# Second layer's attention heads: exponentials and values in rounded halves, all lower halves by VectorE

## What is computed

```python
def one_block(qi):
    s = jnp.einsum('bqhgd,bkhd->bhgqk', qi, k, preferred_element_type=jnp.float32) * scale
    p = jax.nn.softmax(s, axis=-1)
    return jnp.einsum('bhgqk,bkhe->bqhge', p.astype(v.dtype), v)
```

## Time and profile before

| | us |
|---|---|
| median of three runs | 3668.6 (3667.87 to 3674.9) |
| profiled execution, its own time | 3685.8 |
| its span, first to last instruction | 3683.6 |
| heads of the second layer, first score product to last exponential | 2247.2 to 2647.6 |
| TensorE busy | 3453.5 |
| VectorE busy | 1712.7 |
| GpSimd busy | 785.5 |
| ScalarE busy | 734.8 |

### The profile page before, as it was taken

One profiled execution on the slowest core, in us unless ns is written; L12 is line 12 of the kernel. 1 busy time (PEld: TensorE's weight loads), 2 busy tenths in 40 slices (PEclk: granted clock), 3 DMA queues, 4 the chain that ended last, 5 costly groups with the idle time before them and its releaser, 6 DMA issues. The chain is left out here.

```text
span 3683.6 us, 47585 instructions
## 1 busy us (share of the span) xinstructions
PE 3453.5 (94%) x17824; PEld 2975.6 (81%) x17824; DVE 1712.7 (46%) x2862; ACT 734.8 (20%) x1334; POOL 785.5 (21%) x430
## 2 busy tenths in 40 slices
PE   6898899998989999999979988999898999999998
PEld 3787655556889999999969875555587999999998
DVE  1645456663185555555564364333225343333433
ACT  2322243333120000000032123433312000000001
POOL 1211111112222222222113111111221222222220
PEclk8898899999999999999989988999999999999999
DMA  5243433413112222122214334212120111111111
GB/s 186 71 140 108 135 101 111 121 52 88 43 58 77 64 75 68 57 76 65 62 27 134 118 119 101 55 39 58 52 81 29 35 46 46 34 46 40 40 34 51
DMA packets 306201, 271.11 MB, mean 74 GB/s; under 512 B 65778, under 2 KB 268292, under 8 KB 306100
## 3 DMA queue, kind: packets, MB, share of 16 engines
q1 hardware_dynamic: 277492, 234.36, 22.0%
q10 hardware_dynamic: 28608, 35.40, 2.7%
HBM read 221.81 MB, written 48.02 MB: 73 GB/s over the span
## 5 line engine op out<-in xcount | busy, mean ns | idle before, releaser
L1737 PE MATMUL ps<-h_hi,w_hi 128*128 128x384 f32 (+1 forms) x3072 | 1066.5, 347 | 78.2 <-DVE h_lo L1345 63.8
L1738 PE MATMUL ps<-h_lo,w_hi 128*128 128x384 f32 (+1 forms) x3072 | 1045.5, 340 | 0.0
L1739 PE MATMUL ps<-h_hi,w_lo 128*128 128x384 f32 (+1 forms) x3072 | 1045.5, 340 | 0.0
L1737 PEld LDWEIGHTS ps<-h_hi,w_hi 128*128 128x128 f32 (+1 forms) x3072 | 581.2, 189 | 94.2 <-issue 82.8
L1738 PEld LDWEIGHTS ps<-h_lo,w_hi 128*128 128x128 f32 (+1 forms) x3072 | 581.2, 189 | 11.5 <-issue 1.0
L1739 PEld LDWEIGHTS ps<-h_hi,w_lo 128*128 128x128 f32 (+1 forms) x3072 | 580.1, 189 | 3.2
L1658 DVE SCALAR_TENSOR_TENSOR x<-ps,lmod,x 128x384 f32<-128x384 f32 (+2 forms) x768 | 369.5, 513 | 332.9 <-PE ps L1739 332.8
L1562 DVE TENSOR_REDUCE neg_max<-ps 128x1 f32<-128x1152 f32 (+1 forms) x216 | 266.8, 1239 | 275.5 <-PE ps L2013 266.1
L1696 DVE TENSOR_TENSOR wk<-ps,wk 128x384 f32<-128x384 f32 x132 | 73.6, 558 | 688.9 <-PE ps L1739 684.6
L1252 ACT ACTIVATE wk<-ps 128x384 f32<-128x384 f32 x132 | 64.7, 492 | 1498.8 <-PE ps L1739 1482.5
L1186 ACT ACTIVATE p_t<-ps 128x512 f32<-128x512 f32 (+1 forms) x456 | 264.4, 580 | 482.3 <-PE ps L1739 256.0
(11 more groups left out here) (253 smaller groups left out, 4145.7 us busy)
## 6 DMA issues: line engine op xcount, KB each, us to landing
w_stage<-in_w_ffn_gate SPq DMA_DIRECT2D x44, 512.0 KB, 3.7
w_stage<-in_w_ffn_up SPq DMA_DIRECT2D x44, 512.0 KB, 3.8
w_stage<-in_w_ffn_down SPq DMA_DIRECT2D x44, 512.0 KB, 3.6
f_buf<-in_w_ada SPq DMA_DIRECT2D x176, 128.0 KB, 2.1
ada_buf<-in_w_ada SPq DMA_DIRECT2D x36, 512.0 KB, 6.6
s_in<-ev_p ACTq DMA_DIRECT2D x66, 192.0 KB, 2.2
w_stage<-in_w_in SPq DMA_DIRECT2D x24, 512.0 KB, 3.8
ada_w<-in_w_ada SPq DMA_DIRECT2D x4, 2048.0 KB, 17.2
```

The costliest lines, as they stand in the source:

```text
L1737: nc.tensor.matmul(out, wh, xh, start=first, stop=False)
L1738: nc.tensor.matmul(out, wh, xl, start=False, stop=False)
L1739: return nc.tensor.matmul(out, wl, xh, start=False, stop=last)
```

## The change

Only the second layer's heads change (`SPLIT_LAYERS = (1,)`); the first layer keeps its code.

- ScalarE takes two exponentials of each score tile, one written rounded (`p_hi`), one in full (`p_full`), into rings of three slots. TensorE may reuse the scores' bank after the second.
- VectorE subtracts: `p_lo = p_full - p_hi`, once a step (`p_low`). It also rounds and subtracts the values of the next head (`v_halves`, step 3) and makes the lower halves of the next head's queries and keys (`lows`, step 1), which were GpSimd's. The next head's rounding (`highs`) comes in step 0 behind that step's `p_low`; the reductions come one in each of the steps 5 to 13, each ahead of the step's `p_low`.
- TensorE: `products` is two rounded products (upper and lower half of the values by `p_hi`), `product_low` a third (upper half of the values by `p_lo`), issued one step later and behind the next step's `products`.
- GpSimd has nothing in these heads but the weight tiles behind them.
- The loops over pairs in this layer are written out.

```diff
+                    if l in SPLIT_LAYERS:
+                        st = split_step(y, i)
+                        slot = st % 3
+                        if st >= 3:
+                            act.wait_ge(lo_done, st - 2)
+                        nc.scalar.activation(p_hi[:, slot, 0:w], s_bank(half, i)[:, 0:w], ACT.Exp).then_inc(exp_done, 1)
+                        nc.scalar.activation(p_full[:, slot, 0:w], s_bank(half, i)[:, 0:w], ACT.Exp).then_inc(exp_full, 1)
+                        return
...
-                with pool.Fori(0, HEADS) as p:
-                    lows_mla(l * NHEADS + 2 * p)
-                    lows_gqa(l * NHEADS + 2 * p + 1)
+                if l not in SPLIT_LAYERS:
+                    with pool.Fori(0, HEADS) as p:
+                        lows_mla(l * NHEADS + 2 * p)
+                        lows_gqa(l * NHEADS + 2 * p + 1)
...
+                def lows(y, mla):
...
+                    for (lo, full, hi), done in zip(pieces, (q_low, k_low)):
+                        nc.vector.tensor_tensor(lo, full, hi.bitcast(F32), ALU.subtract).then_inc(done, 1)
+
+                def v_halves(p, half, first=False):
...
+                    nc.vector.tensor_copy(hi[:, :, 0:VD], raw[:, :, 0:VD]).then_inc(v_high, 1)
+                    dve.wait_ge(v_high, n + 1)
+                    nc.vector.tensor_tensor(lo[:, :, :], raw[:, :, 0:VD], hi[:, :, 0:VD].bitcast(F32), ALU.subtract)\
+                        .then_inc(v_done, 1)
+
+                def p_low(y, half, i):
...
+                    dve.wait_ge(exp_full, st + 1)
+                    if st >= 3:
+                        dve.wait_ge(pv_mm, y * STEPS + i - 2)
+                    nc.vector.tensor_tensor(p_lo[:, slot, 0:w], p_full[:, slot, 0:w], p_hi[:, slot, 0:w].bitcast(F32),
+                                            ALU.subtract).then_inc(lo_done, 1)
+
+                def pair_split(p, first=False, last=False):
+                    for half in range(2):
+                        y = l * NHEADS + 2 * p + half
+                        more = not (half and last)
+                        for i in range(STEPS):
+                            t = i - MAX_AT - 1
+                            if more and 0 <= t < MAX_TILES:
+                                max_tile(y + 1, t)
+                            p_low(y, half, i)
+                            if more and i == 0:
+                                highs(y + 1, p + half, half == 1)
+                            if more and i == 1:
+                                lows(y + 1, half == 1)
+                            if more and i == 3:
+                                v_halves(p + half, 1 - half, first=first and not half)
...
+                if l in SPLIT_LAYERS:
+                    lows(l * NHEADS, True)
+                    v_halves(0, 0, first=True)
...
                     if not first:
-                        pe.wait_ge(exp_done, st - 1)
+                        if l in SPLIT_LAYERS:
+                            pe.wait_ge(exp_full, split_step(y, i) - 1)
+                        else:
+                            pe.wait_ge(exp_done, st - 1)
...
+                    if l in SPLIT_LAYERS:
+                        _, vh, vl = v_half[half]
+                        slot = split_step(y, i) % 3
+                        nc.tensor.matmul(ps[0:VD + 1, GROUP_BANK[j], 0:w], vh[:, kt, 0:VD + 1], p_hi[:, slot, 0:w],
+                                         start=(i in (0, 9, STEPS - 1)), stop=False)
+                        nc.tensor.matmul(ps[0:VD, GROUP_BANK[j], 0:w], vl[:, kt, :], p_hi[:, slot, 0:w],
+                                         start=False, stop=False)
+                        return
...
+                def product_low(y, half, i):
...
+                    pe.wait_ge(lo_done, split_step(y, i) + 1)
+                    nc.tensor.matmul(ps[0:VD + 1, GROUP_BANK[j], 0:w], v_half[half][1][:, kt, 0:VD + 1],
+                                     p_lo[:, split_step(y, i) % 3, 0:w], start=False, stop=(i + 1 in GROUP_END))\
+                        .then_inc(pv_mm, 1)
...
                             products(y, p, half, i, first and not half)
+                            if l in SPLIT_LAYERS:
+                                if i:
+                                    product_low(y, half, i - 1)
+                                elif half or not first:
+                                    product_low(y - 1, 1 - half, STEPS - 1)
```

More of the change, by code:

```diff
@@ L243 @@
 MACS = 2 * DK
+SPLIT_LAYERS = (1,)
 LATE_HERE = 9
@@ L356, in build @@
             ("neg_max", [P, 16], F32))
+        p_full = place("p_full", [P, 3, 512], F32, ring_at + 4096)
+        p_hi = place("p_hi", [P, 3, 512], F32R, ring_at + 4096 + 3 * 2048)
+        p_lo = place("p_lo", [P, 3, 512], F32R, ring_at + (RING + 1) * 4096)
+        vm_hi, vm_lo, vg_hi, vg_lo = phase(
+            EVB + 6 * T * 4 + 4 * KEYS * 4 + 3 * 1024 + 2 * LAT * 4 + (HL + P) * 4,
+            ("vm_hi", [P, KT, VD + 8], F32R), ("vm_lo", [P, KT, VD], F32R),
+            ("vg_hi", [P, KT, VD + 8], F32R), ("vg_lo", [P, KT, VD], F32R))
+        v_half = ((mv, vm_hi, vm_lo), (gv, vg_hi, vg_lo))
         rope_x, rope_t0, swap = phase(EVB + 6 * T * 4 + 4 * KEYS * 4, ("rope_x", [P, N_ROPE, GW], F32),
@@ L442, in build @@
         f_mac, f_mm, f_ev = sem("f_mac"), sem("f_mm"), sem("f_ev")
+        exp_full, lo_done, v_high, v_done = sem("exp_full"), sem("lo_done"), sem("v_high"), sem("v_done")
         late_mac, late_mm, late_ev = sem("late_mac"), sem("late_mm"), sem("late_ev")
@@ L718, in load_v @@
                 def load_v(hh, dst, src, loaded):
-                    if hh >= 2:
+                    if hh >= 2 and l in SPLIT_LAYERS:
+                        sp.wait_ge(v_done, SPLIT_LAYERS.index(l) * NHEADS + hh - 1)
+                    elif hh >= 2:
                         sp.wait_ge(pv_mm, (l * NHEADS + hh - 1) * STEPS)
@@ L1180, in _, with split_step @@
                 r_store(R_NORMED - 1)
+                def split_step(y, i):
+                    return (y - (l - SPLIT_LAYERS.index(l)) * NHEADS) * STEPS + i
                 def exp_step(y, half, i):
@@ L1226, in _ @@
                 pair(0, first=True)
-                with act.Fori(1, 5) as p:
-                    pair(p)
+                if l in SPLIT_LAYERS:
+                    for p in range(1, 5):
+                        pair(p)
+                else:
+                    with act.Fori(1, 5) as p:
+                        pair(p)
                 pair(5, last=True)
@@ L1598, in ada_sums @@
                             ins.then_inc(late_mac, 1)
-                def pair(p, last=False):
+                def lows(y, mla):
+                    dve.wait_ge(q_high, y + 1)
+                    dve.wait_ge(k_high, y + 1)
+                    if mla:
+                        pieces = ((mq_lo[:, :], qst_m[:, :], mq_hi[:, :]), (mk_lo[:, :], kst_m[:, :], mk_hi[:, :]))
+                    else:
+                        pieces = ((ga[64:P, :], qst_g[64:P, :], ga[64:P, :]),
+                                  (kb[0:64, :], kst_g[0:64, :], ka[0:64, :]))
+                    for (lo, full, hi), done in zip(pieces, (q_low, k_low)):
+                        nc.vector.tensor_tensor(lo, full, hi.bitcast(F32), ALU.subtract).then_inc(done, 1)
@@ new lines, in v_halves @@
+                def v_halves(p, half, first=False):
+                    raw, hi, lo = v_half[half]
+                    n = SPLIT_LAYERS.index(l) * NHEADS + 2 * p + half
+                    dve.wait_ge(vg_loaded if half else vm_loaded, (l * HEADS + p + 1) * 16)
+                    if not first:
+                        dve.wait_ge(pv_mm, (l * NHEADS + 2 * p + half - 1) * STEPS)
+                    nc.vector.tensor_copy(hi[:, :, 0:VD], raw[:, :, 0:VD]).then_inc(v_high, 1)
+                    dve.wait_ge(v_high, n + 1)
+                    nc.vector.tensor_tensor(lo[:, :, :], raw[:, :, 0:VD], hi[:, :, 0:VD].bitcast(F32), ALU.subtract)\
+                        .then_inc(v_done, 1)
@@ new lines, in p_low @@
+                def p_low(y, half, i):
+                    st = (y - (l - SPLIT_LAYERS.index(l)) * NHEADS) * STEPS + i
+                    slot = st % 3
+                    _, w, _ = step_of(i)
+                    dve.wait_ge(exp_full, st + 1)
[3 more added lines that the diff above has]
+                                            ALU.subtract).then_inc(lo_done, 1)
@@ L1601, in pair @@
+                def pair(p, first=False, last=False):
+                    if l in SPLIT_LAYERS:
+                        pair_split(p, first, last)
+                        return
                     for half in range(2):
@@ L1616, in _ @@
                 nc.vector.memset(kst_m[96:97, :], 1.0).then_inc(att_const, 1)
-                nc.vector.memset(mv[:, :, VD:VD + 1], 1.0).then_inc(att_const, 1)
-                nc.vector.memset(gv[:, :, VD:VD + 1], 1.0).then_inc(att_const, 1)
+                for raw, hi, _ in v_half:
```

(34 more changed lines are left out.)

2 lines of the change are left out of this document (added).

## The result

The changed kernel takes 3682.7 us (median of nine, 3681.31 to 3684.93); the kernel before, beside it, 3669.8. The ratio is 1.0029, 95% interval 1.0017 to 1.0041: slower by about 0.3%. The forecast was 3675, and the time lies inside the range of 3662 to 3690; the change itself cost 12.9 us, twice the 6.1 of the sum. The direction and the mechanism in the GQA heads were right; of the terms, several were not.

The account below looks back on a forecast made before the run. TensorE (busy 94%) was taken as the bound, except in the reductions' ring with VectorE. Heads +0.6, entry +2.0 and clock +3.5 us sum to +6.1 on the median 3668.6, say 3675; range 3662 to 3690.

Parts of the forecast that it names:

- The mechanism: In a head's first steps VectorE's queue becomes the bound: TensorE waits for `p_low` 2, until 7.10 us after the first exponential.
- A: From a head's first exponential to its first reduction: 9.76 us forecast in GQA heads (+1.56), 10.20 in MLA heads (+0.83).
- B: The seven 2.24 us intervals between a head's eight large reductions, a ring of VectorE and TensorE; forecast gain and loss 0.
- The fast rival: VectorE is no bound at the head's start, its subtractions running at the pace of casts: 3650 us; chance 10%.
- The pass: On TensorE the full product of the values, 4 × 0.22 us, becomes three rounded ones: one pass of 0.22 less.
- C: From a head's last large reduction to the next head's first exponential: net -0.86 us a head, both kinds.
- VectorE's list in MLA heads: From 1.14 us after the first exponential, 5.96 of VectorE work until `p_low` 2 ends at 7.10; MLA heads net 0.
- The entry: Before the first head's scores, `lows` on VectorE run beside GpSimd's weight splits: 0 to +3.3 us, taken as +2.0.
- The clock: Standstills of 2.2 to 2.4 us in five GQA heads lower TensorE's clock: +3.5 us, bounds 0 and 7.5.
- rival of eleven falls: TensorE's clock falls in each of eleven heads, for longer, once MLA standstills pass some 2 us: 3690 us; chance 12%.
- a ring at half clock: In GQA heads the reductions' ring falls to the lower clock, 3.2 against 2.24 us a step: 3713 us; chance 4%.
- ScalarE: Two exponentials a step take 0.98 us, under TensorE's 1.10 and 1.32; rival, they don't overlap: 3680 us, chance 6%.

## Why the prediction was right, and where it was not

**The mechanism** in the GQA heads is the one forecast. `p_low` 2 of GQA head 7 ended at 7.09 after the first exponential (2502.76 and 0.69, less 2496.36), forecast 7.10; A of GQA heads without a clock fall is 9.77, forecast 9.76. B is unchanged. The spread `lows` took the standstills of both kinds of head away, so the cause is shown and not only argued. The fast rival fell with the widths: the subtractions took 1.35 and 1.49, as forecast.

**The pass: mis-sized.** I took 0.22 for a rounded product and for the pass saved. A product of 64 or 65 columns comes after 0.23, a GQA step lasts 1.16, not 1.10, and the saving is 0.16 a step. I had divided 1.32 by six as if the full form's four passes and the rounded ones were equal; the row was of the full form and of 128-column products only. Hence C gains 0.63 and 0.78 (0.86 forecast) and the last head 2.4 (2.9), about 2.0 us less in all. Of the 0.24 that the late small reduction was to cost, 0.10 came (1.88 less 1.78).

**VectorE's list in MLA heads: mis-sized.** A of MLA heads is 10.47 in place of 10.20, and the pass is not the reason: `p_low` 2 ends at 7.33 after the first exponential (2327.66 and 0.69, less 2321.02), where 7.10 was forecast for both kinds. In the rows of head 2 each of the two `lows` starts 0.03 to 0.04 behind its predecessor's end, and not 0.09 ahead of it, as the sum had it and as head 7 shows. Why is not shown. It costs 1.3 us in five heads.

The base has a share too: heads 7 and 8, from which A was read, had 8.20 and 9.37, but heads 1 and 3 had 8.04, and heads 2 and 10 9.18. In sum the five GQA heads cost 5.0 without the clock (3.5 forecast), the five MLA heads behind the first 1.9 (0), and the last head gave 2.4 (2.9): 4.0 us, of which 2.0 are the pass, 1.3 this list and the rest the base.

**The entry: mis-sized most.** The forecast was +2.0 with an upper bound of 3.3, for `lows` ahead of the first scores. That delay is 0.3: TensorE's wait for the first scores grew from 1.36 to 1.69. But head 0, which the sum put at nothing, lost 4.7. The collision was named, with the right row, but priced for `lows` only. (In that row VectorE's subtraction ended 0.42 behind the split, not with it.) The splits ran for 13.3 us (each has a cast of 1.04 or more ahead of the subtraction, and they too became longer: 3.49 against 2.40), so `v_halves` and the first `p_low` behind `lows` ran into them too. The upper bound had to be the whole of what VectorE queues until the last split ends. Part of head 0's times is the clock's lower level at the entry: A before is 9.86 here, and 9.17 with half reductions, where the level had risen earlier.

The Trainium skill, "SBUF — State Buffer", section "SBUF: two separate sides", says that there is a shared pair of ports, which VectorE, in a two-port mode or (against a GpSimd operation that reads SBUF) with two SBUF inputs, and GpSimd take for a whole instruction while the other waits. The trace agrees: 2.87 for a `p_low` beside a subtraction of 2.84, and 0.69 with the splits moved away.

**The clock: near in size, in part by luck.** Forecast 3.5 with bounds 0 and 7.5, for five GQA heads. It fell in two of them, at 1.35 and 1.48 each (11.12 and 11.25 less 9.77), and in head 0, where I had not looked; none fell in MLA heads behind 1.04. The price of one fall was near (at most 1.5 forecast, 0.9 to 1.6 measured with the run that has the splits behind the heads); that 3.5 came near is luck, since the forecast did not say in how many heads it falls. The standstill is 1.90 in the record, not the 2.2 to 2.4 forecast. The step that failed is to go by the length of the standstill: 1.89 or 1.90 brought the fall in heads 0, 3 and 7 of one execution and 1, 3 and 7 of another, and 3.39 with 1.89 behind it brought none in the run with half reductions. What picks the heads stays open. The rival of eleven falls and that of a ring at half clock did not come; the ring ran at full clock with some 0.6 of standstill in 2.24.

**ScalarE** was no bound behind the ring: the second exponential starts 0.49 behind the first (2496.36, 2496.85), as in the earlier trace rows, and the exponentials ended none of TensorE's waits in the steps there; only the spread order brought that about, by `max_row`. Ahead of the ring they ended one that the kernel before did not have, 0.56 in each MLA head behind the first, here in head 8:

```profile
2536.25 0.44 PE L2094 MATMUL ps<-p_hi,vm_hi 128*65 128x512 f32 x1 [0.56 <-ACT p_hi L1208]
```

In the changed kernel the wait for `p_lo` comes behind it and hides it. It remains where `lows` are moved: A of MLA heads is then 9.2, hardly less than before, though TensorE's list is shorter. No run was made to take that wait away.

In sum the stage took +12.2 and the entry ahead of it +0.3, forecast +6.1. Of the difference 4.0 are the pass, VectorE's list in MLA heads and the base, and 3.0 the entry with head 0 (4.7 and 0.3 against 2.0), less 0.7 for the clock in GQA heads (2.8 against 3.5). The range held because its upper end had the bounds of clock and entry in it.

## What to carry to other kernels

When an engine is given more work, write its queue out in order from the moment that its first consumer needs something, and put whatever is needed late (here a lower half that is first read sixteen steps on) behind what is needed now: the same work, moved from step 1 to steps 13 and 15, took back the whole loss of 0.3%; with the queries' half first and GpSimd's splits behind the heads it became a gain of 0.4%. Then ask who else waits for the moved operation: the queries' half had a second reader on ScalarE. And where work is taken off GpSimd, look at what starts in its place, and beside which VectorE operations, down to the end of that work.

## What the runs showed of the hardware that was not expected

A full float32 product of 65 weight columns costs 0.86 per 512 columns (1.32 less two of 0.23), three rounded ones 0.69 to 0.70: the split saves 0.16 and not a whole pass. Two equal standstills of 1.90 us in equal heads of one execution left the granted clock at 2.4 GHz in one and brought it to 1.2 GHz for about three microseconds in the other; in another run it stayed at 2.4 GHz behind 3.39 us.
